# RWKV recurrence of a hybrid layer trunk: back part of one head pair beside the inverse of the next, inverse in 32x32 blocks, products in pairs on four quarters of the array

## The reference

```python
def step(S, inp):
    r_t, w_t, k_t, v_t, kk_t, b_t = inp
    sa = jnp.einsum('bhvk,bhk->bhv', S, -kk_t)
    S = S * w_t[:, :, None, :] + sa[..., None] * b_t[:, :, None, :] + v_t[..., None] * k_t[:, :, None, :]
    return S, jnp.einsum('bhvk,bhk->bhv', S, r_t)
S_fin, y = lax.scan(step, wkv_prev.astype(f32), (tm(rh), tm(wh), tm(kh), tm(vh), tm(kk), tm(bh)))
```

## Time and profile before

| | |
|---|---|
| Median of 3 runs | 3362.47 us |
| The profiled execution | 3362.26 us |
| Its span, first to last instruction | 3360.5 us |
| TensorE busy, over the span | 2986.1 us (89%) |
| VectorE, ScalarE, GpSimd busy | 39%, 33%, 4% |
| Mean granted TensorE clock | 0.957 |

### The profile page before, as it was taken

The page is one execution under the profiler, slowest core; times in us unless marked ns, Lnnn a source line. Parts: engine busy times, 40 slices in busy tenths (PEclk is TensorE's granted clock), DMA queues, the critical chain, the costliest instruction groups (busy, mean ns, idle before and its releaser), DMA issues. The chain is left out here.

```text
span 3360.5 us, 81805 instructions
## 1 busy us (share of the span) xinstructions
PE 2986.1 (89%) x37120; PEld 2782.1 (83%) x37120; DVE 1318.7 (39%) x2139; ACT 1124.8 (33%) x1557; POOL 130.6 (4%) x123
## 2 busy tenths in 40 slices
PE   5999999999688888888859948999999999996993
PEld 4999999999677777777759928999999999996993
DVE  4343333221355665566521154343333334333113
ACT  5343333322144343343322233333333333333221
POOL 0000000000000000000000010000000000000001
PEclk8999999999799999999979968999999999997997
DMA  2333333332111111111132153222232222223222
GB/s 107 105 105 112 112 112 112 112 112 100 43 48 44 42 45 43 45 42 44 37 133 88 47 191 128 77 95 80 87 103 80 87 88 88 91 78 118 76 84 97
DMA packets 91238, 288.85 MB, mean 86 GB/s; under 512 B 18721, under 2 KB 25249, under 8 KB 70433
## 3 DMA queue, kind: packets, MB, share of 16 engines
q1 hardware_dynamic: 79136, 257.19, 22.3%
q10 hardware_dynamic: 9216, 17.83, 1.4%
q0 software_dynamic: 2560, 8.91, 0.7%
HBM read 229.56 MB, written 54.34 MB: 84 GB/s over the span
## 5 line engine op out<-in xcount | busy, mean ns | idle before, releaser
L134 PE MATMUL ab_pair<-ab_x_hi,ab_w_hi 128*128 128x272 f32 x2048 | 432.9, 293 | 23.9 <-ACT ab_x_hi L303 19.2
L1225 PE MATMUL e_pair<-e_x_hi,e_w_hi 128*128 128x272 f32 x1984 | 442.2, 304 | 6.4 <-DVE e_w_lo L1500 6.4
L134 PE MATMUL ab_pair<-ab_x_hi,ab_w_lo 128*128 128x272 f32 x2048 | 425.5, 289 | 0.0
L134 PE MATMUL ab_pair<-ab_x_lo,ab_w_hi 128*128 128x272 f32 x2048 | 424.3, 289 | 0.0
L1225 PE MATMUL e_pair<-e_x_hi,e_w_lo 128*128 128x272 f32 x1984 | 415.2, 291 | 0.0
L1225 PE MATMUL e_pair<-e_x_lo,e_w_hi 128*128 128x272 f32 x1984 | 414.3, 291 | 0.0
L346 DVE TENSOR_TENSOR ab_w_lo<-ab_raw,ab_w_hi 128x2048 fp32r<-128x2048 f32 x64 | 146.6, 2293 | 524.2 <-ACT ab_w_hi L278 524.2
L134 PEld LDWEIGHTS ab_pair<-ab_x_hi,ab_w_hi 128*128 128x128 f32 x2048 | 325.9, 189 | 29.6 <-issue 21.0
L1225 PEld LDWEIGHTS e_pair<-e_x_hi,e_w_hi 128*128 128x128 f32 x1984 | 313.4, 191 | 39.3 <-issue 32.0
L134 PEld LDWEIGHTS ab_pair<-ab_x_lo,ab_w_hi 128*128 128x128 f32 x2048 | 323.6, 190 | 0.0
L134 PEld LDWEIGHTS ab_pair<-ab_x_hi,ab_w_lo 128*128 128x128 f32 x2048 | 321.7, 190 | 0.0
(11 more groups left out here) (327 smaller groups left out, 4799.1 us busy)
## 6 DMA issues: line engine op xcount, KB each, us to landing
ab_raw<-in_w_in SPq DMA_DIRECT2D x64, 1024.0 KB, 4.8
e_raw<-in_hgrn_in SPq DMA_DIRECT2D x64, 1024.0 KB, 4.8
o_raw<-in_rwkv_wo SPq DMA_DIRECT2D x16, 1024.0 KB, 4.8
o_raw<-in_hgrn_wo SPq DMA_DIRECT2D x16, 1024.0 KB, 4.7
o_o<-scr_yz SPq DMA_DIRECT2D x32, 272.0 KB, 9.0
e_Ss<-in_hgrn_s SPq DMA_DIRECT2D x16, 512.0 KB, 4.7
out_hgrn_s<-e_Sd SPq DMA_DIRECT2D x16, 512.0 KB, 7.0
ab_nxt<-in_x SPq DMA_DIRECT2D x4, 1088.0 KB, 9.2
```

The costliest lines, as they stand in the source:

```text
L134: mm = pe.matmul(out[:, a, 0:TH], w, x[:, kt, a * TH:(a + 1) * TH], start=(kt == 0 and n == 0), stop=(kt == KT - 1 and n == 2))
L1225: mm = pe.matmul(out[:, a, 0:TH], w, x[:, kt, a * TH:(a + 1) * TH], start=(kt == 0 and i == 0), stop=(kt == KT - 1 and i == 2))
```

## The change

- The inverse is built in blocks of 32 x 32 only: new tiles pTiT, pTi and pX of 128 x 256 hold, for each chunk and head, the two diagonal blocks of the 64 x 64 matrix. `level_x` and `level_yt` use four 32 x 32 matmuls per chunk, each on its own 32 rows and 32 columns of the array, and there are four levels. The fifth is replaced by a corner: `corner_x` and `corner_yt` compute the off-diagonal 32 x 32 block; GpSimd (`diagonal`) writes the diagonal blocks into TiT and ScalarE (`corner`) copies the corner in. Masks and adds of VectorE work on 256 columns.
- `strict` computes MT with 32-column weights, interleaved with Mak.
- Products come in pairs: `channel_pair` and `token_pair` interleave two products. One reads a head's rows and writes the same head's rows, the other writes (or reads) the other head's, so that the four matmuls of a chunk use all four quarters of the array, and the two products go to different PSUM banks. Paired are Btok with Ktok, Atok with Vtok, Mrb with Mrk, R0 with TA, G with the value part of y, U0 with the value part of the states. For this PSUM has six tiles l, c0, c1, f, y, m beside q.
- The order of all engines is new. The loop runs over i from -2 to 15, with j = i + 1 and h = i + 2: the inverse of pair j is interleaved with the state chain of pair i, the sample recurrence of a pair moves to its back part, and the normalisation of k (`square_sum`, Ln, Exp, `kkn`) and the w product (`rank_w`) are done a pair ahead, for h. `kt_` and `kkn` have two buffers. ScalarE's list of functions is now Sigmoid, Exp, Ln, Exp, Ln, Exp per pair (before: Ln, Sigmoid, Exp, Ln, Exp).
- VectorE's order in an iteration is: scan(j), mrk(i), three sample_u(i) between kf, csx and k2 of j, rk(j), g(i), bb, kt, bt of j, rhoe(i), at(j), first states and link 1 of i, bv(j), snew(i), link 2, tit0, MT, turn_ti 0 of j, link 3, ssm(h), mask_x 1, mak, link 4, add and turn 1, link 5, mask_x 2, link 6, add and turn 2, kkn(h), the small sample operands, mask_x 3, rho(j), add and turn 3, mask_x 4, sMs, mrb, add and turn 4, yn(i), link 7, yb(i), the copy to pX for the corner, yz(i).

The diff, cut to its core:

```diff
-        names = ["reset", "bones", "center", "strict", "incl", "eye", "lev1", "s_mask", "seq"]
-        names += [f"lev{m}" for m in RWKV_LEVELS[1:]]
+        names = ["reset", "bones", "center", "strict", "incl", "eye", "strict32", "s_mask", "seq", "h_diag", "h_lev1", "bdiag"]
+        names += [f"p_lev{m}" for m in RWKV_LEVELS[1:5]]
...
-        lev = [tables[f"lev{m}"] for m in RWKV_LEVELS]
-        NL = len(RWKV_LEVELS)
+        lev = [k.h_lev1] + [tables[f"p_lev{m}"] for m in RWKV_LEVELS[1:5]]
+        NL = len(RWKV_LEVELS) - 1
+        HC = C // 2
...
-        MT, Mak, Mrb, Mrk, TiT, Ti, X = (sb(n, [P, SEQ]) for n in ("MT", "Mak", "Mrb", "Mrk", "TiT", "Ti", "X"))
+        MT, Mak, Mrb, Mrk, TiT = (sb(n, [P, SEQ]) for n in ("MT", "Mak", "Mrb", "Mrk", "TiT"))
+        pTiT, pTi, pX = (sb(n, [P, SEQ // 2]) for n in ("pTiT", "pTi", "pX"))
...
-        b0, b1, y_ps, m_ps = (ps(n, [P, 512]) for n in ("b0", "b1", "y", "m"))
-        s = R.sems("const_in r_in k_in v_in z_in w2_in S0_in zeroed "
+        l_ps, c0_ps, c1_ps, f_ps, y_ps, m_ps = (ps(n, [P, 512]) for n in ("l", "c0", "c1", "f", "y", "m"))
...
+                    if j >= 0:
+                        sp.wait_ge(s.lora_a, j + 1)
+                    sp.dma_start(w2[:, 1, :], d.w2[1][h]).then_inc(s.w2a_in, 16)
+                if h + 1 < KT:
+                    if j >= 0:
+                        sp.wait_ge(s.ksq, j + 1)
+                        sp.wait_ge(s.kkn, j + 1)
+                        sp.wait_ge(s.k2, j + 1)
+                    load_k(h + 1)
...
+                        sp.wait_ge(s.Sd, i + 1)
+                        sp.wait_ge(s.sy_mm, i + 1)
+                    sp.dma_start(S0[:, :, :], d.wkv[j]).then_inc(s.S0_in, 16)
+                if h < KT:
+                    if j >= 0:
+                        sp.wait_ge(s.rk, j + 1)
+                        sp.wait_ge(s.rho, j + 1)
+                    sp.dma_start(rt[:, :], d.rkvz[0][h]).then_inc(s.r_in, 16)
+                    if j >= 0:
+                        sp.wait_ge(s.bv, j + 1)
+                        sp.wait_ge(s.av_mm, j + 1)
+                        sp.wait_ge(s.sm_mm, j + 1)
+                    sp.dma_start(vt[:, :], d.rkvz[2][h]).then_inc(s.v_in, 16)
+                if h + 1 < KT:
+                    sp.wait_ge(s.lora_w, h + 1)
+                    load_w2w(h + 1)
...
+            def quarter(out, o_half, lhsT, rhs, i_half, start=True, stop=True):
+                return pe.matmul(out[rows(o_half)], lhsT[rows(i_half)], rhs[rows(i_half)], start=start, stop=stop,
+                                 skip_group_check=not (start and stop))
...
-            def chunks(out, lhsT, rhs, c0=0):
-                for c in range(c0, NCH):
-                    mm = stacked(cut(out, c), cut(lhsT, c), cut(rhs, c))
+            def channel_pair(same, l_same, r_same, swapped, l_swap, r_swap):
+                for c in range(NCH):
+                    for hh in range(2):
+                        quarter(cut(same, c), hh, cut(l_same, c), r_same if r_same is k.eye else cut(r_same, c), hh)
+                        mm = quarter(cut(swapped, c), 1 - hh, cut(l_swap, c),
+                                     r_swap if r_swap is k.eye else cut(r_swap, c), hh)
                 return mm
 
-            def by_token(out, src):
+            def token_pair(same, l_same, r_same, c0, swapped, l_swap, r_swap, keep_open):
                 for c in range(NCH):
-                    mm = stacked(cut(out, c), cut(src, c), k.eye)
+                    for hh in range(2):
+                        mm = quarter(cut(swapped, c), hh, cut(l_swap, c), cut(r_swap, c), 1 - hh,
+                                     c == 0 or not keep_open, not keep_open)
+                        if c >= c0:
+                            mm = quarter(cut(same, c), hh, cut(l_same, c), cut(r_same, c), hh)
                 return mm
...
+            def strict(j):
+                a, b = at[j % 2], bt
+                pe.wait_ge(s.at, j + 1)
+                pe.wait_ge(s.bt, j + 1)
+                pe.wait_ge(s.kt, j + 1)
+                if j:
+                    pe.wait_ge(s.rhoe, j)
+                    pe.wait_ge(s.state, NCH * (j - 1) + 1)
+                for c in range(NCH):
+                    for hh in range(2):
+                        for half in range(2):
+                            at0 = c * C + HC * half
+                            pe.matmul(cut(c1_ps, c)[q32(2 * hh + half)], b[rows(hh), at0:at0 + HC],
+                                      a[rows(hh), at0:at0 + C], start=True, stop=True)
+                        mm = quarter(cut(f_ps, c), 1 - hh, cut(kt, c), cut(a, c), hh)
+                mm.then_inc(s.strict_mm, 1)
...
             def level_x(j, l):
-                pe.wait_ge(s.ti, (NL - 1) * j + l)
-                chunks(b1, MT, Ti).then_inc(s.x_mm, 1)
+                pe.wait_ge(s.ti, NL * j + l)
+                if l == 1 and j:
+                    pe.wait_ge(s.corner, 2 * j)
+                if l == 1:
+                    pe.wait_ge(s.MT, j + 1)
+                for c in range(NCH):
+                    for g in range(4):
+                        mm = pe.matmul(half_cut(l_ps, c)[q32(g)], MT[q32(g), c * C:c * C + HC],
+                                       half_cut(pTi, c)[q32(g)], start=True, stop=True)
+                mm.then_inc(s.x_mm, 1)
 
...
             def level_yt(j, l):
-                pe.wait_ge(s.X, (NL - 1) * j + l)
-                chunks(b0, X, TiT).then_inc(s.yt_mm, 1)
-
...
+                pe.wait_ge(s.X, NL * j + l)
+                for c in range(NCH):
+                    for g in range(4):
+                        mm = pe.matmul(half_cut(l_ps, c)[q32(g)], half_cut(pX, c)[q32(g)],
+                                       half_cut(pTiT, c)[q32(g)], start=True, stop=True)
+                mm.then_inc(s.yt_mm, 1)
+
+            def corner_x(j):
+                pe.wait_ge(s.ti, NL * j + 5)
+                for c in range(NCH):
+                    for hh in range(2):
+                        mm = pe.matmul(half_cut(l_ps, c)[rows(hh)], cut(MT, c)[q32(2 * hh)],
+                                       half_cut(pTi, c)[q32(2 * hh)], start=True, stop=True)
+                mm.then_inc(s.x_mm, 1)
+
+            def corner_yt(j):
+                pe.wait_ge(s.X, NL * j + 5)
+                for c in range(NCH):
+                    for hh in range(2):
+                        mm = pe.matmul(half_cut(l_ps, c)[q32(2 * hh)], half_cut(pX, c)[q32(2 * hh + 1)],
+                                       half_cut(pTiT, c)[q32(2 * hh + 1)], start=True, stop=True)
+                mm.then_inc(s.yt_mm, 1)
...
+                channel_pair(c1_ps, bt, k.eye, f_ps, kt, k.eye).then_inc(s.bk_mm, 1)
...
+                channel_pair(c1_ps, at[j % 2], k.eye, f_ps, vt, k.eye).then_inc(s.av_mm, 1)
...
+                channel_pair(c1_ps, bt, rho, f_ps, kt, rho).then_inc(s.incl_mm, 1)
...
+                token_pair(c1_ps, TiT, Atok, 1, c0_ps, Mak, Vtok, False).then_inc(s.r0ta_mm, 1)
...
+                token_pair(c1_ps, TA, Btok, 1, y_ps, Vtok, Mrk, True).then_inc(s.g_mm, 1)
...
+                token_pair(c0_ps, TiT, R0, 0, f_ps, Ktok, Vtok, True).then_inc(s.u0_mm, 1)
...
+            for i in range(-2, KT):
+                j, h = i + 1, i + 2
+                back, front, ahead = i >= 0, 0 <= j < KT, h < KT
+                if front:
+                    rank_a(j)
+                if back:
+                    sample_step(i, 0)
+                    first_right(i)
+                    sample_step(i, 1)
+                    sample_step(i, 2)
+                    g_and_value_y(i)
+                    u_and_value_state(i)
+                if front:
+                    bonus(j)
+                if back:
+                    rho_rest(i)
+                    u_state(i)
+                    sample_states(i)
+                    chain(i, 1)
...
+                if front:
+                    strict(j)
+                if back:
+                    chain(i, 2)
+                if ahead:
+                    square_sum(h)
+                if back:
+                    chain(i, 3)
+                    sample_y(i)
+                if front:
                     level_x(j, 1)
+                if back:
+                    u_y(range(4, NCH))
+                    state_y(i, 3)
+                    chain(i, 4)
+                    state_y(i, 2)
+                    state_y(i, 1)
+                if front:
                     level_yt(j, 1)
+                    b_and_k_by_token(j)
+                if back:
+                    chain(i, 5)
+                if front:
                     level_x(j, 2)
                 if back:
+                    u_y(range(0, 4))
+                    chain(i, 6)
+                    state_y(i, 4)
+                    state_y(i, 6)
+                if front:
                     level_yt(j, 2)
+                if back:
+                    state_y(i, 7)
+                    state_y(i, 5).then_inc(s.y_mm, 1)
```

(79 more changed lines are left out.)

559 lines of the change are left out of this document (280 added, 279 removed).

## The result

The changed kernel takes 3433.7 us (median of 4 runs, 3412.7 to 3440.8) beside 3362.1 for the kernel before on the same chip: ratio 1.020, 95% interval 1.0153 to 1.0248, so slower by more than the noise, but not clearly by 2%. Forecast was 3101 us. The profiled execution took 3430.4 us, its span 3428.6.

What follows compares the result with a forecast made beforehand. TensorE was taken to bound the kernel: terms of 32.0 us a pair, 32.6 with waits. Stage 49 + 15 x 32.6 + 35 = 573 us against 834.5, so 3362.3 us became 3101; own range 3075 to 3130, chance 0.55.

Steps and rivals of the forecast that it cites:

- term (e): TensorE's `strict`, 96 instructions with narrower weights: 1.0 us a pair, bound 2.8 us at 29 ns each.
- Term (g): TensorE's changes between shapes: 0.08 us into the 32-column shape, 0.14 out, eleven excursions, 2.4 us a pair.
- a floor per instruction: Rival: 29 ns is the instruction supply's floor in a long stream; +18.0 us, period 50.6, time 3371; chance 0.06.
- the 8.8 ns burst: Evidence against a supply floor: HGRN product, 32-column weights on four column groups, 32 instructions in 0.28 us.
- never lets a queue fill: Caveat in the supply rival: 1344 matmuls with their weight loads in 33 us leave no queue of ready instructions.
- (d): TensorE's six paired products on four quarters: 376 instructions at 14.5 ns, 5.5 us a pair, bound 10.9.
- the rival of two quarters: Rival: matmuls on the same columns never run together; +6.4 us, period 39.0, time 3197; chance 0.25.
- (f): TensorE's eight level products of 64 instructions, 32 weight columns: 8 x 0.56 = 4.5 us a pair; corner_yt 0.5.
- ping-pong: TensorE and VectorE alternating in the inverse; its staying, period 45 to 50, was excluded as a whole.
- chain of waits: Rival: one operand late each iteration, behind ScalarE's loads or slowed rk; period 34 to 37, 3122 to 3167; chance 0.10.
- The six table loads: Expected sign: six ScalarE table loads a pair, one more than before, at 1.28 us.
- GpSimd slowing VectorE in a rival: Within the waits rival: VectorE's rk comes late, slowed by GpSimd at work beside it; one to four us new waiting.

Runs made afterwards that it cites:

- x1: Changed kernel with strict's 64 narrow (32-column) instructions issued first and its 32 wide ones after, instead of alternating; 3290.2 us, ratio 0.9768.
- x5: Changed kernel with strict's narrow instructions before the wide ones within each chunk, one change of shape per chunk instead of two; 3324.4 us, ratio 0.9873.
- b1: Kernel before, with its first strict product cut into narrow instructions and alternating with the second as in the changed kernel; 3551.8 us, ratio 1.0552.
- x4: x1 with every level_yt product issued twice on the same operands, 256 more instructions a pair; 3423.2 us, ratio 1.0165.
- x3: x1 with the two products of each of the six pairs issued one behind the other; 3305.7 us, ratio 0.9812.
- x8: x1 with 64 moving columns instead of 32 in the level_yt products, no instruction added; 3287.2 us, ratio 0.9776.

## Why the prediction was wrong, point by point

**The step that failed: term (e), `strict` at 1.0 us with a bound of 2.8.** It measured 9.4 us in the mean of the 14 pairs, 10.3 in the pair shown. I priced 96 instructions and forgot their order. Term (g) counted eleven excursions between whole products; inside `strict` the shape changes 31 times. The duration I used for one, 0.08 in and 0.14 out, was low by a quarter (0.15 either way), but the count was the main error: 31 changes at my own price would have been 3.4 us. 16 rounds of 0.49 us would be 7.8 at full clock, of which 2.1 are the instructions themselves (x1); the lower clock makes 9.4 of it. The Trainium skill (TensorEngine Tiling (Array Packing), Key Properties) says that changing the tiling mode drains TensorE. The traces agree: a change takes 0.15 us from start to start, where sorted instructions start 16 ns apart (narrow) or some 30 (wide, x1).

**The clock was not in the sum.** All rows before were at full clock. After, the 14 pairs run at 0.81, and the full-array product behind `strict` shows 2.18 us where x1's shows 1.18. What the rows show of it: it was 1.00 when this `strict` began and 0.50 for the rest of it. Fewer changes go with a higher clock (0.90 in x1 and x5). In its 14 pairs the clock falls 26 times. 14 of these falls are inside `strict`, one in each pair, and b1, which has the same mixed product in the old kernel, shows the same 14 and no other. 11 of the other 12 come during a wait for a packet of 1.2 to 2.1 us or within 2.5 us after it. x1, without the mixing, has 18 falls in its 14 pairs, none in `strict`, 17 of them behind such a wait (1.4 to 2.1 us). x4, with longer waits (1.40 us in the mean against 1.23), has 33; x3, with shorter ones (1.08), has 5. So both causes of lost time also bring the clock down, and about two thirds of the changed kernel's time at the lower clock (195 of 294 us) begin inside `strict`.

**The rival "a floor per instruction" held the second cause, in the wrong form.** I let it cost 29 ns for each instruction of the narrow and paired products, and held the 8.8 ns burst against it. Bursts do run at 8.8 and 14.5 ns. The limit is on the stream: a packet for 127 matmuls and their weight loads every 3.3 us at best, 4.2 us as x4 prices it. 1344 / 127 x 3.3 = 34.9 us, already above the 32.6 forecast, and at x4's 4.2 us a packet 44.4, where x1 has 44.3. What sets the 3.2 us between two packets at the least, no run shows. Before, 1062 instructions in 49.65 us asked for a packet every 6 us, and the limit never showed. The sentence that the stream "never lets a queue fill" was right; I gave it 0.06. That matmul starts stay 25 ns apart, as the Trainium skill has it (TensorE: Matmul & The Clock Gate, Part 1), the traces contradict start by start, though on the mean of this stage an instruction costs more than that.

**How the 20.5 us between 32.6 and 53.1 divide**, estimated from rows: `strict` 9.4 - 1.0 = 8.4; TensorE's waits named "issue" in the 14 pairs, summed, 65.2 / 14 = 4.7; the lower clock outside `strict`: 38% of 53.1 is 20.2 us, of which 4.7 in `strict`, so 15.5 us at half speed, which lose 7.7 at most. Together 20.8. The last is an upper bound, since a slower array also leaves the supply more time.

**What held.** Four quarters work at once: (d) at 14.5 ns, the rival of two quarters is out. (f), the levels, as assumed. No ping-pong: TensorE waits for c_pTi once in the 14 pairs (the matmuls 0.7 us, the weight loads 0.9), where the weight loads waited 71.9 for Ti in the stage before. No chain of waits for ScalarE or VectorE sets the period. The six table loads are there and hidden. The end took 37.0 us against 35, and the first strict product began 27.4 us into the stage against 27. The start took 938.6 - 871.2 = 67.4 us against 49, with the same `strict` in it. VectorE's three operations on yc take 1.2 to 1.5 us each instead of 0.7 to 0.8. In 15 of the 16 pairs GpSimd is at work beside them, and in the last, where it is not, they take 0.78, 0.78 and 0.72: the prediction had GpSimd slowing VectorE in a rival, but not here. No wait of TensorE shows it.

## What to carry to other kernels

Write out the order of instructions inside a product before you price it: the count of shape changes is as much a term as the count of instructions, and sorting by shape is free (143 us here for one loop split in two). When work is cut into smaller products that run side by side, check the rate of the instruction stream over microseconds, not the rate in a burst: here some 27 ns at best and 33 ns in practice for a matmul with its weight load, below which faster products mostly make gaps that the profile calls "issue". To tell such a gap from others, number the engine's records: waits for instructions recur at the same place of every packet. In such a stream wider operands cost little (x8) and additional instructions cost more than their own work (x4).

## What the runs showed of the hardware

- A change between 64x32 and 64x64 weights: 0.15 us from start to start at full clock (changed kernel, x5), 0.24 at the lower; four and two instructions in 0.49 us, 0.75 at the lower clock.
- Four 64x64 quarters at once: 14.5 ns a matmul. 32x32 blocks: 8.8 ns with 32 moving columns. 64x32 weights on two row halves: 16 ns.
- Instruction packets of 16 KB for 127 matmuls with weight loads, never under 3.2 us apart in the recurrence, 4.2 in the mean of x1; TensorE starts 1.2 to 1.6 us behind a landing when it had to wait. Added instructions cost 34 ns each with what the clock adds (x4, clock 0.82); added moving columns cost nothing in the sum (x8, clock 0.94).
- The granted clock fell to 1.2 GHz in `strict` while the profile showed TensorE 100% busy, in every pair of the changed kernel and of b1: busy time by modelled ends says little of what the array does in a stretch full of shape changes.
- VectorE operations of 0.72 to 0.78 us take 1.2 to 1.5 us with GpSimd at work beside them (the operations on yc).
